# Two transformer blocks: the hidden rows of the FFNs turned by VectorE and DRAM instead of by TensorE

## The reference

```python
def swiglu(h, w_gu, w_down):
    g, u = jnp.split(h @ w_gu, 2, axis=-1)      # w_gu: 1024 x 5632
    return (jax.nn.silu(g) * u) @ w_down        # w_down: 2816 x 1024
```

## Time and profile before

| | |
|---|---|
| median of 3 runs | 1354.86 us (1354.81 to 1355.17) |
| span of the profiled execution | 1354.2 us; its own time outside the span isn't recorded, the median is 0.7 us longer |
| TensorE busy | 1339.0 us, 99% |
| VectorE busy | 930.6 us, 69% |
| ScalarE busy | 749.4 us, 55% |
| moved by DMA | 270.89 MB, mean 200 GB/s |

### The profile page before, as it was taken

The page is one execution under the profiler, slowest core; times in us unless marked ns, Lnnn a source line. Parts: engine busy times, 40 slices in busy tenths (PEclk is TensorE's granted clock), DMA queues, the critical chain, the costliest instruction groups (busy, mean ns, idle before and its releaser), DMA issues.

```text
span 1354.2 us, 17190 instructions
## 1 busy us (share of the span) xinstructions
PE 1339.0 (99%) x6599; PEld 1117.7 (83%) x6599; DVE 930.6 (69%) x1334; ACT 749.4 (55%) x1169; POOL 67.2 (5%) x132
## 2 busy tenths in 40 slices
PE   9999999999999999999999999999999999999998
PEld 6888888888888888888788888889988888788886
DVE  6677867856656777877767787678866455755553
ACT  6444448567864544446845444766457664744442
POOL 3100100000000000010000010100000000000000
PEclk9999999999999999999999999999999999999999
DMA  9888866543376678885577885665544355556662
GB/s 282 290 262 277 310 199 190 167 117 108 100 243 195 214 252 272 289 288 167 168 245 250 279 290 150 202 173 159 168 140 112 108 172 169 166 180 184 187 190 88
DMA packets 167057, 270.89 MB, mean 200 GB/s; under 512 B 14242, under 2 KB 114826, under 8 KB 166976
## 3 DMA queue, kind: packets, MB, share of 16 engines
q1 hardware_dynamic: 154240, 226.66, 53.8%
q0 software_dynamic: 12576, 43.06, 9.5%
q10 hardware_dynamic: 160, 0.07, 0.0%
HBM read 268.66 MB, written 1.05 MB: 199 GB/s over the span
## 4 chain that ended last, share of the span: by engine, by line
PE 94%; DVE 3%; ACT 1%; DMA 1%; issue 0%; POOL 0%; DVEq 0%; SPq 0%; ACTq 0%
PE ps L1982 25%; PE ps L1947 16%; PE ps L1949 16%; PE ps L1948 16%; PE ps L2171 2%; PE ps L1961 1%; PE ps L2182 1%; PE ps L1962 1%; PE ps L1963 1%; PE ps L2065 1%; PE ps L2067 1%; PE ps L2066 1%; PE ps L2488 1%; PE ps L1997 1%; PE ps L2086 1%; PE ps L2255 1%
## 5 line engine op out<-in xcount | busy, mean ns | idle before, releaser
L1151 DVE TENSOR_TENSOR w_lo<-raw,w_hi 128x1024 fp32r<-128x1024 f32 (+2 forms) x431 | 515.1, 1214 | 249.1 <-ACT w_hi L636 246.9
L636 ACT ACTIVATE w_hi<-raw 128x1024 fp32r<-128x1024 f32 (+2 forms) x431 | 448.5, 1054 | 330.5 <-DMA raw<-in_ffn_wgu_dram 92.8
L1947 PE MATMUL ps<-w_hi,a_hi 128*128 128x512 f32 (+1 forms) x976 | 390.5, 400 | 1.1 <-DVE w_lo L1151 0.8
L1949 PE MATMUL ps<-w_hi,a_lo 128*128 128x512 f32 (+1 forms) x976 | 379.5, 389 | 0.0
L1948 PE MATMUL ps<-w_lo,a_hi 128*128 128x512 f32 (+1 forms) x976 | 378.5, 388 | 0.0
L1949 PEld LDWEIGHTS ps<-w_hi,a_lo 128*128 128x128 f32 x976 | 183.3, 188 | 38.8
L1947 PEld LDWEIGHTS ps<-w_hi,a_hi 128*128 128x128 f32 x976 | 183.6, 188 | 36.1 <-DVE w_lo L1151 1.0
L1948 PEld LDWEIGHTS ps<-w_lo,a_hi 128*128 128x128 f32 x976 | 183.8, 188 | 34.6
L1982 PE MATMUL ps<-w_hi,hid_hi 128*128 128x512 f32 x300 | 93.5, 393 | 0.0
L1982 PE MATMUL ps<-w_lo,hid_hi 128*128 128x512 f32 x300 | 92.5, 390 | 0.0
L1982 PE MATMUL ps<-w_hi,hid_lo 128*128 128x512 f32 x300 | 92.5, 390 | 0.0
(11 more groups left out here) (433 smaller groups left out, 1640.4 us busy)
## 6 DMA issues: line engine op xcount, KB each, us to landing
raw<-in_ffn_wgu_dram SPq DMA_DIRECT2D x176, 256.0 KB, 4.2
raw<-in_w_in_dram SPq DMA_DIRECT2D x88, 512.0 KB, 3.7
raw<-in_w_gu_dram SPq DMA_DIRECT2D x176, 256.0 KB, 3.3
ada<-in_w_ada_dram POOLq DMA_DIRECT2D x72, 512.0 KB, 5.4
raw<-in_ffn_wdown_dram SPq DMA_DIRECT2D x44, 512.0 KB, 4.6
raw<-in_w_dn_dram SPq DMA_DIRECT2D x44, 512.0 KB, 4.3
raw<-in_w_in_dram SPq DMA_DIRECT2D x36, 256.0 KB, 3.1
raw<-in_w_out_dram SPq DMA_DIRECT2D x16, 512.0 KB, 4.1
```

The source lines that it names most:

```text
L636: act.activation(w_hi[:, u % RING, 0:nk * n], raw[:, u % RING, 0:nk * n], ACT.Copy).then_inc(hi_ready, 1)
L1151: dve.tensor_tensor(w_lo[:, u % RING, 0:nk * n], raw[:, u % RING, 0:nk * n], w_hi[:, u % RING, 0:nk * n].bitcast(F32), ALU.subtract).then_ ...
L1947: pe.matmul(dst(t)[:, 0:n], a[0], slot(u, w_hi, kk, n), start=kc == 0, stop=False)
L1949: i = pe.matmul(dst(t)[:, 0:n], a[1], slot(u, w_hi, kk, n), start=False, stop=kc == KC - 1)
```

## The change

TensorE no longer turns hidden values. VectorE turns each block in 32x32 pieces with one instruction straight after making it. Two blocks make a pair (m; 6 groups an FFN, the last with one block). SyncE writes a pair from SBUF to the output tensor in DRAM, used as scratch until the end, and reads it back with four loads of 32 partitions each, so that the pieces land in the right place. ScalarE and VectorE split a pair at once, from SBUF and no longer from PSUM. The write stands ahead of the load of up unit 19 + 8m, the reads 6 and 7 loads later; for groups 4 and 5 they stand ahead of down loads 12, 14, 15 and 16, 18, 19. Groups 0 to 2 are split in blocks 5, 7 and 9, group 3 at down unit 6, group 4 at 14, group 5 at 18, behind the gate's low part and, on TensorE, needed at down unit 18. In block 10 the modulation products move behind the turn. The modulation sum behind down unit 4 moves behind unit 6. Two pairs of semaphores of the start become one pair, and `hid` is single instead of double.

```diff
+            def gather_hidden(f, m, part, parts):
+                n = min(2, UPB - 2 * m)
+                if part == 0:
+                    sp.wait_ge(sem("blocks_turned"), f * UPB + min(2 * m + 2, UPB))
+                    sp.dma_start(passed(m)[:, :, 0:n], turned(m)[:, :, 0:n]).then_inc(sem("blocks_passed"), 16)
+                if part >= parts - 2:
+                    sp.wait_ge(sem("blocks_passed"), 16 * (HGROUPS * f + m + 1))
+                    dst = gathered(m).rearrange("p (i b) -> p i b", i=4)
+                    src = passed(m)[:, :, 0:n].rearrange("(i u) q b n -> q u i (b n)", i=4)
+                    for q in range(2 * (part - parts + 2), 2 * (part - parts + 2) + 2):
+                        sp.dma_start(dst[32 * q:32 * q + 32], src[q]).then_inc(sem(f"gathered{m % 2}"), 16)
...
+                if u in gather_at:
+                    gather_hidden(*gather_at[u])
                 load_unit(u)
@@ ScalarE, ffn_part
-                    if j >= 1:
-                        hidden_hi(f, j - 1)
+                    if j >= 5 and j % 2 == 1:
+                        hidden_hi(f, (j - 5) // 2)
...
-                w.to(dn + 5)
-                hidden_hi(f, UPB - 1)
+                w.to(dn + 6)
+                hidden_hi(f, HGROUPS - 3)
+                w.to(dn + 14)
+                hidden_hi(f, HGROUPS - 2)
...
+                w.to(dn + 18)
+                hidden_hi(f, HGROUPS - 1)
@@ VectorE, ffn_part
-                    if j >= 1:
-                        hidden_lo(f, j - 1)
+                    if j >= 5 and j % 2 == 1:
+                        hidden_lo(f, (j - 5) // 2)
...
                     i.then_inc(sem("hid_ready"), 1)
+                    turn_blocks(f, j)
+                    if f < 3 and j == UPB - 1:
+                        ada_products(ADA_F * f + ADA_AT[j], ADA_AT[j + 1] - ADA_AT[j])
...
                 w.to(dn + 5)
-                hidden_lo(f, UPB - 1)
                 for n in range(4):
                     if f < 3:
                         ada_products(ADA_F * f + ADA_AT[UPB] + 2 * n, 2)
+                    if n == 0:
+                        w.to(dn + 6)
+                        hidden_lo(f, HGROUPS - 3)
                     w.to(dn + 8 + 3 * n)
+                    if n == 2:
+                        hidden_lo(f, HGROUPS - 2)
...
                 if f < 3:
                     gate_lo(f)
+                w.to(dn + 18)
+                hidden_lo(f, HGROUPS - 1)
...
+            def turn_blocks(f, j):
+                dve.wait_ge(sem("hid_ready"), f * UPB + j + 1)
+                before = HGROUPS // 2 * f + j // 4
+                if j % 2 == 0 and before > 0:
+                    dve.wait_ge(sem(f"gathered{j // 2 % 2}"), 64 * before)
+                dve.transpose(turned(j // 2)[:, :, j % 2, :].rearrange("p q (b u) -> p q b u", u=32),
+                              hid[:, :, :, :].rearrange("p c t (q u) -> p q (c t) u", u=32)).then_inc(sem("blocks_turned"), 1)
@@ TensorE, ffn_part
-                        if j >= 1 and i == (2 if j == 1 else 1):
-                            turn_hidden(f, j - 1)
...
-                    if k == 2:
-                        turn_hidden(f, UPB - 1)
-                    pe.wait_ge(sem("hid_lo_ready"), f * UPB + k // 2 + 1)
+                    pe.wait_ge(sem("hid_lo_ready"), HGROUPS * f + k // 4 + 1)
...
-                    if k == 4:
+                    if k == 6:
                         sum_mods(FFN[f], UPB)
```

More of the change, by code:

```diff
@@ L215, in two_blocks @@
         hid_hi, _, e = place("hid_hi", [P, FC, S], F32R, ARENA)
-        hid_lo, _, e = place("hid_lo", [P, FC, S], F32R, e)
+        hid_raw, HR0, _ = place("hid_raw", [P, FC * S], F32, e)
+        hid_lo, _, e = place("hid_lo", [P, FC, S], F32R, HR0)
         HB = e
@@ L219, in two_blocks @@
         sg, _, e = place("sg", [P, 2, T, HALF], F32, HB)
-        hid, _, END = place("hid", [P, 2, T, HALF], F32, e)
+        hid, _, e = place("hid", [P, 2, T, P], F32, e)
+        turned_even, _, END = place("turned_even", [P, 4, 2, P], F32, e)
+        turned_odd, _, _ = place("turned_odd", [P, 4, 2, P], F32, KD0)
         assert END <= nc.sbuf_usable_end, (END, nc.sbuf_usable_end)
@@ L290, in acc, with turned, passed, gathered @@
             return ps[:, 2 * t + s, :]
+        def turned(m):
+            return turned_odd if m % 2 else turned_even
+        def passed(m):
+            return out[0, m % 2 * P:(m % 2 + 1) * P, :].rearrange("p (q b n) -> p q b n", q=4, n=P)
+        def gathered(m):
+            at = 4 * S * (m + 1 if m < HGROUPS - 2 else m - HGROUPS + 2)
+            return hid_raw[:, at:at + min(4, FC - 4 * m) * S]
+        def by_piece(v, m):
+            return v[:, 4 * m:min(4 * m + 4, FC), :].rearrange("p c (t n) -> p (c t) n", t=T).rearrange("p b (i u) -> p b i u", u=32)
         def wide(t):
@@ L523, in load_unit @@
                     sp.dma_start(dst[:, :, n // 2:n], src[1]).then_inc(landed[u % RING], 16)
+            def gather_hidden(f, m, part, parts):
[9 more added lines that the diff above has]
+                        sp.dma_start(dst[32 * q:32 * q + 32], src[q]).then_inc(sem(f"gathered{m % 2}"), 16)
+            gather_at = {}
+            for f in range(4):
+                at = ffn[f][0] + RING + 11
+                for m in range(HGROUPS):
+                    parts = 8
+                    if m >= HGROUPS - 2:
+                        parts = 4
+                        at = ffn[f][1] + RING + 4 * (m - HGROUPS + 3)
+                    for part in range(parts):
+                        gather_at[at] = (f, m, part, parts)
+                        at += 1
             xs = A["x"][0].rearrange("(t p) d -> p t d", p=P)
@@ L1402, in ffn_part, with hidden_lo @@
                 w.to(dn + FC + (1 if f == 2 else 2))
[L1404 to L1407, removed]
+            def turn_blocks(f, j):
[5 more added lines that the diff above has]
+                              hid[:, :, :, :].rearrange("p c t (q u) -> p q (c t) u", u=32)).then_inc(sem("blocks_turned"), 1)
+            def hidden_lo(f, m):
+                dve.wait_ge(sem("hid_hi_ready"), HGROUPS * f + m + 1)
+                if m >= 1:
+                    dve.wait_ge(sem("hid_lo_ready"), HGROUPS * f + m)
+                dve.tensor_tensor(by_piece(hid_lo, m), gathered(m).rearrange("p (i b u) -> p b i u", i=4, u=32), by_piece(hid_hi, m).bitcast(F32), ALU.subtract)\
+                   .then_inc(sem("hid_lo_ready"), 1)
             def ada_products(i0, n):
@@ L1599, in _ @@
                 dve.memset(m[:, :], 1.0).then_inc(sem("mask_ready"), 1)
[L1600 to L1602 removed]
+            dve.wait_ge(sem("params_turned"), 1)
+            dve.tensor_copy(gain0[:, :], ps[:, 1, 0:KC]).then_inc(sem("params_ready"), 1)
+            dve.wait_ge(sem("params_ready"), 1)
             turned_lo("f0", units_between=True)
@@ L2174, in first_down @@
                             i.then_inc(used, 1)
[L2176 to L2183, removed]
             def sum_mods(key, j):
@@ L2352, in _ @@
             pe.wait_ge(sem("gain0_landed"), 16)
-            pe.transpose(ps[:, 1, 0:KC], grow8[:, :], ident[0:KC, 0:KC]).then_inc(sem("gain0_turned"), 1)
+            pe.transpose(ps[:, 1, 0:KC], grow8[:, :], ident[0:KC, 0:KC]).then_inc(sem("params_turned"), 1)
             turn("f0", x, (0,))
```

36 lines of the change are left out of this document (17 added, 19 removed).

## The result

The changed kernel took 1362.0 us (median of 4 runs, 1359.9 to 1363.7) against 1354.8 for the kernel before on the same chip: a ratio of 1.0051, 95% interval 1.0036 to 1.0065. It is **slower by 0.5%** (7 us), where the prediction said 1336.0 us, 1333 to 1346, faster.

A forecast was written before the change was run, and what follows sets the result against it. TensorE, busy 99% of the span, was taken to bound the kernel. 1354.86 us less 21.1 for the hidden transposes plus 2.2 for the gate's products, all else nothing, gave 1336.0 us, range 1333 to 1346.

The forecast's parts named there:

- TensorE's term: Over four FFNs TensorE loses 44 turns of four hidden transposes at 0.48 us, a gain of 21.1 us.
- VectorE, ScalarE, SyncE's queue: Added VectorE transposes (+32 us net), fewer ScalarE copies and SyncE's added issues and waits were each to cost nothing.
- the last write's landing: SyncE's wait for the last groups' write, 2 units (5.4 us) after it; a 256 KB store landed in 2.0 us.
- DMA bytes: Hidden rows' traffic beside the weight loads adds 48 GB/s; first FFN's queue falls 5.9 us behind, cost to TensorE 0.
- the double price: Rival, 16%: 32-partition reads of hidden rows take twice a weight's time per byte; 10.4 us more, 1346 us.
- The sum by rates: Per FFN, DMA rate needed against room: 338 against 316 GB/s in the first, 320 against 325, 314 against 327.
- the cushion: Weights are split 6 to 12 us early; VectorE or DMA may lag that much within one FFN before TensorE notices.
- The gate's products: After down row 14 they wait for the modulation row's low part, made later: 2.2 us stall, from 0 to 5.

The follow-up runs named there:

- e13: e12 with the gate's four products moved from behind down unit 14 to behind down unit 17 in three FFNs: 1334.6 us (0.9850).
- e2: The changed kernel with each write and read carrying a quarter of the bytes in a quarter of the pieces, other work kept: 1339.0 us (0.9874).
- e4: The changed kernel with the last group's write issued three loads earlier, ahead of down load 13: 1368.7 us (1.0097).
- e3: The kernel before with the change's writes and 32-partition reads added at the same places, data unused, nobody waiting: 1384.1 us (1.0197).
- e7: e3 with each of the four reads going to all 128 partitions, same bytes and pieces: 1358.3 us (1.0028).
- e12: The changed kernel with the block exchange moved to four writes a group from 32 partitions, each read reaching 128 partitions: 1343.6 us (0.9910).

## Why the prediction was wrong

*TensorE's term was right.* 21.1 us forecast, 21.1 by the unit starts, and e13 ends 20.7 us under the 1355.3 of its chip.

*VectorE, ScalarE, SyncE's queue: nothing.* Right. The turn takes 0.71 us where I took 0.7 (line of the changed kernel below), and e2, which keeps all this work, takes 1339.0. I had the last write's landing wrong by its size (15 us, not 2.0), but e4, without SyncE's wait for it, was no faster.

```profile
L1468 DVE STREAM_TRANSPOSE turned_even<-hid 128x512 f32<-128x512 f32 x24 | 17.1, 711 | 0.8
```

*DMA bytes: here it failed, in two steps.* I priced the hidden rows at the rate of weights, 48 GB/s, and gave the double price 16% and 10.4 us as a rival. The dearer price is what holds (1.95 times, e3 against e7), and its cost was mis-sized: taking it away gives 18.4 us in the changed kernel (e12), 26 in the kernel before (e7). The sum by rates went wrong too: it gave a lag of 5.9 us in f0 and none in f1 and f2, at double price 12.4, 5 and 2.9, and down unit 15 was 8.2, 8.2 and 6.1 us late. Why f1 and f2 lag as much as f0, with the DMA share at 0.94 in f1's up stage, no run here shows. The second step is the cushion. I let a lag of about 6 us vanish in the 6 to 12 us by which weights are ahead of TensorE. That held for TensorE's own units but for 0.5 us in f0. But the modulation's low part stands behind the same loads in VectorE's order, and its spare time was in my own rows: 1.2, 0 and 2.3 us. Most of a lag of 6 to 8 us therefore had to come out.

*The gate's products: 2.2 us forecast, from 0 to 5; measured 24.4.* I counted only the step and the issues newly put ahead of them, 1 to 2.5 us, and not the lag. Nor did I count that an idle TensorE loses its clock, 5.6 us of the 24.4. Even with wide reads (e12) the three idles are 6.5 us, and e13 is 9.0 faster than e12. Of the 27.4 us between the changed kernel and e13, about two thirds are narrow reads and one third is the place of the products; taken in the other order the shares turn round (20.6 for the place, then 6.8), since either alone hides much of the other.

*Start of the down stage in f0: nothing forecast, 3.0 lost.* TensorE has three idles there, 1.45, 0.74 and 0.48 us:

```profile
132.77 0.47 PE L2234 MATMUL ps<-w_hi,hid_hi 128*128 128x512 f32 x1 [1.45 <-issue]
...
136.50 0.50 PE L2234 MATMUL ps<-w_hi,hid_hi 128*128 128x512 f32 x1 [0.74 <-DVE hid L1433]
...
145.43 0.70 PE L2051 MATMUL ps<-w_hi,hid_hi 128*128 128x512 f32 x2 [0.48 <-DVE w_lo L1200]
```

The first two are waits for the hidden rows of blocks 9 and 10, which VectorE made late, at 132.67 and 136.44: it had waited 1.7 us for a weight at 124.67 and has no idle from there to 136.44. So they are the late loads again, and with wide reads (e12) they are gone. Only the third comes from the change's own waits. VectorE's turn of block 10 waits 1.9 us for the reads of group 3, which were issued at 126.30, began at 126.77 and landed 11.5 us later. The chain of the changed kernel:

```profile
126.77 11.47 DMA hid_raw<-out_dram
...
138.34 0.06 DVE turned_odd L1468
```

I had asked whether reads pass without delay for those who split them, and not for the buffer that the next turn reuses.

## What to carry to other kernels

Price a transfer by its form and not by its bytes: how many partitions the side in SBUF has, and how large the outermost dimension is, before comparing it with a queue that is already 80% busy. When a queue falls behind, don't look for the cushion of the main stream alone; look for every step that stands behind the same loads in some engine's order and has the least spare time. A step with 1.2 us of spare turned a lag of 8.2 us into 8.2 of idle, since another 1.1 us of work had been put ahead of it, and 10.0 with the clock.

## What was not expected of the hardware

- Receiving in 32 partitions held the DMA engines 1.6 to 2.1 times as long as receiving in 128 (49.3 to 64.8 against 31.4 us; 1.95 in e3 against e7). Sending from 32 cost about 28.4 us against 24.7, by subtraction and with smaller pieces: far from double. The Trainium skill (SBUF — State Buffer, section Door 1: The DMA port swizzle) gives half the ports for a span of 32, which agrees with the receiving side; it makes no difference between the directions, and e12 does.
- A source whose outermost dimension is 4 left 4 closing packets a read in place of 16, and 11.5 MB of such reads, which nobody needed, cost 54 us.
- Moving one write, so that waits of 24 us in all went from the queue that issues loads, made the kernel 6.7 us slower (e4); why isn't shown.
- After an idle of 8.2 us TensorE's gate products are 0.43 us apart, where they are 0.24 apart in e13, and the granted clock is 0.76 over the next 5 us.
